# Two transformer blocks in float32: the second block's heads taken two by two, and the linear attention's pair mask stored for its diagonal blocks only

## The reference, cut to what matters

```python
# gated linear attention, per chunk of 64 tokens
diff = bcum[:, :, :, None, :] - bcum[:, :, None, :, :]
decay = jnp.exp(jnp.where(mask[:, :, None], diff, -jnp.inf))
att = jnp.einsum('bhtd,bhsd,bhtsd->bhts', qc, kc, decay)
o_intra = jnp.einsum('bhts,bhse->bhte', att, vc)

# second block: A, 4 heads: the difference of two softmaxes with width 64
w = p[0] - lam * p[1];   oa = rms_norm(w @ v)
# B, 8 heads: a window of 128 tokens, with a sink
# C, 8 heads: three attentions (selected, window, compressed blocks), each with its own gate
out = g[..., 0:1] * o_cmp + g[..., 1:2] * o_sel + g[..., 2:3] * o_win
gate = jax.nn.sigmoid(mg)          # 3 x 1024 gates for each token
x = x + jnp.sum(gate * y, axis=2) @ w_out
```

## Time and profile before

| | us |
|---|---|
| median of 3 runs | 4096.61 |
| lowest and highest | 4095.42, 4098.13 |
| the profiled execution's own time | 4089.71 |
| its span, first to last instruction | 4087.9 |

### The profile page before, as it was taken

One profiled execution on the slowest core, in us unless ns is written; L12 is line 12 of the kernel. 1 busy time (PEld: TensorE's weight loads), 2 busy tenths in 40 slices (PEclk: granted clock), 3 DMA queues, 4 the chain that ended last, 5 costly groups with the idle time before them and its releaser, 6 DMA issues. The chain is left out here.

```text
span 4087.9 us, 51442 instructions
## 1 busy us (share of the span) xinstructions
PE 3835.9 (94%) x19551; PEld 3010.5 (74%) x19551; DVE 1891.2 (46%) x2849; ACT 1006.2 (25%) x1824; POOL 1965.8 (48%) x834
## 2 busy tenths in 40 slices
PE   7999999999988998899999999899899999999999
PEld 4777778888877887676678778677585555567877
DVE  3344336556547884244426556456214444463200
ACT  3333112222210001243312222101214444412200
POOL 3333342332335564344454443689443333287886
PEclk9999999999999998999999999999889999999999
DMA  6211221121125553222232222335422222253333
GB/s 207 50 44 48 75 50 42 44 50 42 45 75 118 115 106 108 72 55 56 55 85 55 63 61 51 89 91 140 123 57 69 64 55 68 62 159 78 93 92 92
DMA packets 485314, 317.41 MB, mean 78 GB/s; under 512 B 38185, under 2 KB 456370, under 8 KB 483210
## 3 DMA queue, kind: packets, MB, share of 16 engines
q1 hardware_dynamic: 466080, 288.14, 28.6%
q10 hardware_dynamic: 19050, 26.75, 1.9%
HBM read 282.25 MB, written 32.56 MB: 77 GB/s over the span
## 5 line engine op out<-in xcount | busy, mean ns | idle before, releaser
L945 POOL TENSOR_TENSOR whi<-ring,con 128x1024 fp32r<-128x1024 f32 (+1 forms) x415 | 980.1, 2362 | 2067.1 <-DMA ring<-in_w_in 1596.5
L622 PE MATMUL ps<-xT_parts,whi 128*128 128x512 f32 (+2 forms) x2632 | 1017.2, 386 | 71.7 <-DVE zz L2235 21.1
L622 PE MATMUL ps<-hT_parts,whi 128*128 128x512 f32 (+1 forms) x2864 | 1049.9, 367 | 0.0
L947 POOL TENSOR_TENSOR ring_parts<-ring,whi 128x1024 fp32r<-128x1024 f32 (+1 forms) x415 | 988.9, 2383 | 32.5
L622 PE MATMUL ps<-xT_parts,ring_parts 128*128 128x512 f32 (+2 forms) x2600 | 946.2, 364 | 0.0
L622 PE MATMUL ps<-arena_parts,whi 128*128 128x512 f32 (+1 forms) x2344 | 723.0, 376 | 50.5 <-DVE arena_parts L2267 37.0
L1659 ACT ACTIVATE arena<-ps 128x768 f32<-128x768 f32 (+9 forms) x561 | 298.7, 542 | 1625.9 <-PE ps L622 786.0
L622 PE MATMUL ps<-arena 128*128 128x128 f32 (+9 forms) x3292 | 644.6, 340 | 13.0 <-DVE arena L2235 9.5
L622 PEld LDWEIGHTS ps<-xT_parts,whi 128*128 128x128 f32 (+1 forms) x2632 | 501.2, 190 | 179.0 <-issue 87.9
L622 PEld LDWEIGHTS ps<-hT_parts,whi 128*128 128x128 f32 x2864 | 544.3, 190 | 89.6 <-issue 7.2
L622 PEld LDWEIGHTS ps<-arena 128*128 128x128 f32 (+3 forms) x3292 | 440.4, 194 | 168.3 <-issue 131.4
(11 more groups left out here) (173 smaller groups left out, 3617.7 us busy)
## 6 DMA issues: line engine op xcount, KB each, us to landing
ring<-in_w_in SPq DMA_DIRECT2D x504, 256.0 KB, 4.1
arena<-in_w_ada SPq DMA_DIRECT2D x64, 256.0 KB, 5.8
ring<-in_w_up SPq DMA_DIRECT2D x64, 256.0 KB, 4.0
ring<-in_w_down SPq DMA_DIRECT2D x64, 256.0 KB, 3.9
ring<-in_w_out SPq DMA_DIRECT2D x48, 256.0 KB, 3.9
gates_kept<-stage ACTq DMA_DIRECT2D x24, 384.0 KB, 3.9
arena<-gates_kept SPq DMA_DIRECT2D x24, 384.0 KB, 3.6
arena<-in_w_ada SPq DMA_DIRECT2D x8, 1024.0 KB, 20.0
```

The lines of the kernel that those rows point to most:

```text
L622: return nc.tensor.matmul(o, l, r, start=first, stop=last)
L945: v.tensor_tensor(hi, raw, ones[:, 0:m].unsqueeze(1).to_broadcast([P, kt, m]), ALU.mult).then_inc(w_rounded, 1)
L947: v.tensor_tensor(ringR[:, s, 0:kt, 0:m], raw, hi.bitcast(F32), ALU.subtract).then_inc(w_split, 1)
```

## The change

It does two things.

**1. Linear attention.** `pairs` is stored without its zero blocks (448 columns for each direction instead of 1024). `levels` makes one 64x64 matmul for the first halving, into bank 6, and then for the six others and the diagonal two matmuls each of 64 weight columns and 64 moving columns, one for each half, into 448 columns of bank 5. It waits for `att_ready` besides `masked`. `mask` multiplies 448 columns, sums over seven, spreads the 64 columns to the two blocks by a product with `blk`, and copies the corner.

**2. Heads.** Group 0 and group 1 of the same query tile now stand next to each other in `heads2`, and all engines go through it two scores at a time. `scores` issues two matmuls in a row, then come fill steps, the two turns, the values, and fill steps again. `values` takes both groups in turn, matmul by matmul, and sel and win apart. `pT2` has another layout with room for four uses. The planner works by pairs. Gate 0's tile is made before the first score, and its weights are loaded before SyncE waits for the phase "cmp" and issues the bias tables. The gates are kept as sigmoids, made with Exp, Ln and Exp instead of Tanh, so that one table serves the stage and it is loaded once before the heads; the branch stage then multiplies by the gate alone.

```diff
-        pairs.append(k.transpose(1, 0, 2).reshape(P, -1))
+        own_pairs = np.concatenate([k[1:8, :64, :64], k[1:8, 64:, 64:]], axis=1)
+        pairs.append(own_pairs.transpose(1, 0, 2).reshape(P, -1))
...
-            for kind, g, subs in (("A", 0, ("c",)), ("B", 0, ("b",)), ("B", 1, ("b",)),
-                                  ("C", 0, ("sel", "win", "cmp")), ("C", 1, ("sel", "win", "cmp"))):
...
+            for kind, sub, groups in (("A", "c", (0,)), ("B", "b", (0, 1)), ("C", "sel", (0, 1)), ("C", "win", (0, 1)),
+                                      ("C", "cmp", (0,)), ("C", "cmp", (1,))):
+                for qt in range(LT):
...
+                    for g in groups:
...
-        VALUES_AT = [("A", 0, 8, 2), ("B", 0, 17, 2), ("B", 1, 19, 2), ("C", 0, 28, 3), ("C", 1, 40, 3)]
+        VALUES_AT = [("A", 8, 2), ("B", 16, 2), ("sel", 24, 2), ("win", 32, 2), ("cmp0", 36, 1), ("cmp1", 40, 1)]
...
-        FILL_TILES, gates_planned = [], 0
+        FILL_TILES, gates_planned = [], 1
...
+            for p in range(pairs_):
+                spent += sum(pair_us(2 * p))
+                room = int((share * (p + 1) - spent) / step_us)
+                for slot in range(2):
+                    for _ in range(room - room // 2 if slot == 0 else room):
+                        if at == steps or 2 * p + slot < free:
+                            break
...
+                            ends[tile] = p
+                            free = 2 * p + (4 if FILL_TILES[tile][0] == "query" else 2)
...
                     for c in range(4):
                         load_query(0, c)
+                    load_gate(0)
...
                             pe.wait_ge(masked, f0 + f)
+                            pe.wait_ge(att_ready, f0 + f)
+                            halves = [slice(0, 64), slice(64, P)]
+                            keys_of = [gkE[:, j % 2, lv * P:(lv + 1) * P] for lv in range(LEVELS)]
+                            queries_of = [gqE[:, j % 3, lv * P:(lv + 1) * P] for lv in range(LEVELS)]
+                            mm(bank(6, 64)[halves[d]], keys_of[0][:, halves[d]], queries_of[0][:, halves[1 - d]], True, True)
+                            keys_of.append(gk[:, t * P:(t + 1) * P])
+                            queries_of.append(gq[:, t * P:(t + 1) * P])
                             for lv in range(LEVELS):
-                                mm(bank(5, 1024)[:, lv * P:(lv + 1) * P], gkE[:, j % 2, lv * P:(lv + 1) * P],
-                                   gqE[:, j % 3, lv * P:(lv + 1) * P], True, True)
-                            mm(bank(5, 1024)[:, 7 * P:8 * P], gk[:, t * P:(t + 1) * P], gq[:, t * P:(t + 1) * P],
-                               True, True).then_inc(att_done, 1)
+                                for half in halves:
+                                    last = mm(bank(5, LEVEL_COLS)[half, lv * 64:(lv + 1) * 64], keys_of[lv + 1][:, half],
+                                              queries_of[lv + 1][:, half], True, True)
+                            last.then_inc(att_done, 1)
...
-                mm(b, q, k, True, True).then_inc(scores2, 1)
+                return score_bank(n, u["w"]), q, k
+
+            def scores(n):
+
+                for b, q, k in [operands(n + c) for c in range(2)]:
+                    mm(b, q, k, True, True).then_inc(scores2, 1)
...
+                elif kind in ("sel", "win"):
+                    for s in range(LT):
+                        for g in range(2):
+                            todo.append((bank(1)[rows[g], s * P:], (vS if kind == "sel" else vW)[:, s, rows[g]],
+                                         pT_keys(use[g], s, s * P, LAT - s * P), kind == "sel" and s == 0, False))
...
-                        pe.wait_ge(gate2_tanh, before.count("gate"))
+                        pe.wait_ge(gate2_read, 1 + before.count("gate"))
...
+            pe.wait_ge(w_split, splits.number() + 1)
+            for k in range(KT):
+                fill_step(k)
             pe.wait_ge(n2_ready, NORM0 + 4)
...
+            scores(0)
+            for n in range(0, 4 * NS2 + 2, 2):
+                if n + 2 < 4 * NS2:
+                    scores(n + 2)
                 fill(n)
-                for q in ended(n - 1, "query"):
+                for m in (n, n + 1):
+                    if m < 4 * NS2:
+                        turn(m)
+                for m in (n, n + 1):
+                    for kind, first, steps in VALUES_AT:
+                        j, o = divmod(m - first, NS2)
+                        if 0 <= j < 4 and o < steps:
+                            values(j, kind, o, steps)
+                fill(n + 1)
+                for q in ended(n // 2 - 1, "query"):
                     pe.wait_ge(fill_kept, q + 1)
                     pe.wait_ge(sq2_ready, NORM0 + 4 + q + 1)
                     mm(bank(2), blk, n2sq, True, True).then_inc(ms2_done, 1)
...
+            log_and_exp_table()
             for c in range(4):
                 normed2(NORM0 + c)
...
+            def gate_value(g):
+
+                product()
+                if g >= 2:
+                    act.wait_ge(gate2_kept[g % 2], 16 * (g // 2))
+                value = gate_out2[g % 2]
+                do(value, bank(2).rearrange("p (a n) -> p a n", a=2), ACT.Exp, scale=-1.0).then_inc(gate2_read, 1)
+                act.wait_ge(gate2_read, g + 1)
+                do(value, value, ACT.Ln, bias=one).then_inc(gate2_ln, 1)
+                act.wait_ge(gate2_ln, g + 1)
+                do(value, value, ACT.Exp, scale=-1.0).then_inc(gate2_ready, 1)
+                tiles.next()
...
+            gate_value(0)
             exp(0)
             exp(1)
+            keep_gate2(0)
+            for n in range(0, 4 * NS2, 2):
...
-                    log_and_exp_table()
...
+                for g in ended(n // 2 - 1, "gate"):
+                    gate_value(g)
+                if n + 2 < 4 * NS2:
+                    exp(n + 2)
+                    exp(n + 3)
                 copy(n)
...
+                copy(n + 1)
...
-                        v.tensor_tensor(gam, bank(5, 1024).rearrange("p (l t) -> p l t", l=8), pairs[:, d],
-                                        ALU.mult).then_inc(masked, 1)
+                        v.tensor_tensor(gam, bank(5, LEVEL_COLS), pairs[:, d], ALU.mult).then_inc(masked, 1)
                         dve.wait_ge(masked, f0 + f + 1)
+                        own(v.tensor_reduce(gdiag, gam.rearrange("p (l t) -> p t l", l=LEVELS), AX.X, ALU.add))
+                        own.settle()
 
                         dve.wait_ge(o_done, f0 + max(f - 1, 0))
-                        v.tensor_reduce(gatt[:, f % 2], gam.rearrange("p l t -> p t l"), AX.X, ALU.add).then_inc(att_ready, 1)
+                        own(v.tensor_tensor(gatt[:, f % 2].rearrange("p (c t) -> p c t", c=2),
+                                            gdiag.unsqueeze(1).to_broadcast([P, 2, 64]),
+                                            blk.rearrange("p (c t) -> p c t", c=2), ALU.mult))
+                        own.settle()
+                        rows, cols = slice(64 * d, 64 * d + 64), slice(64 * (1 - d), 64 * (1 - d) + 64)
+                        v.tensor_copy(gatt[rows, f % 2, cols], bank(6, 64)[rows]).then_inc(att_ready, 1)
...
+            for n in range(0, 4 * NS2, 2):
                 i, m = divmod(n, NS2)
+                normalise(n)
+                normalise(n + 1)
                 if n + 2 < 4 * NS2:
                     maximum(n + 2)
-                normalise(n)
+                    maximum(n + 3)
...
-                release(stt(pieces[0], gate_in2[g % 4], 1.0, pieces[1], ALU.add, ALU.mult))
+                release(v.tensor_tensor(pieces[0], gate_in2[g % 4], pieces[1], ALU.mult))
```

More of the change, by code:

```diff
@@ L38 @@
 SUM_COLS = LEVEL_COLS + 2 * 128
-CON_ROOM = 2 * (9 * 128 - SUM_COLS)
+CON_ROOM = 2 * (9 * 128 - SUM_COLS) + 2 * (8 * 128 - LEVEL_COLS)
 NEG = -1e30
@@ L136 @@
 for _n, _w in (("ident", P), ("ones", P), ("blk", P), ("anti", P), ("rot", P), ("cos", LAT), ("sin", LAT),
-               ("sums", 2 * SUM_COLS), ("pairs", 2 * 8 * P), ("room", CON_ROOM)):
+               ("sums", 2 * SUM_COLS), ("pairs", 2 * LEVEL_COLS), ("room", CON_ROOM)):
     C_AT[_n] = (_at, _w)
@@ L566, in two_blocks, with pair_us @@
                     gates_planned += 1
[L568 to L579, removed]
+        def pair_us(n):
+            scores = 2 * (heads2[n + 2]["w"] / 1200 + 0.1) if n + 2 < 4 * NS2 else 0.0
+            others = 0.0
+            for m in (n, n + 1):
+                if m < 4 * NS2 and heads2[m]["sub"] != "c0":
+                    others += 0.1 + 0.11 * -(-heads2[m]["w"] // P)
+                for kind, first, steps in VALUES_AT:
+                    j, o = divmod(m - first, NS2)
+                    if 0 <= j < 4 and o < steps:
+                        others += {"A": 1.1, "B": 0.6, "sel": 0.7, "win": 0.7}.get(kind, 0.9)
+            return scores, others
@@ L581, in planned_fill @@
         def planned_fill():
-            step_us, units = 0.7, 4 * NS2 - 4
```

(26 more changed lines are left out.)

152 lines of the change are left out of this document (71 added, 81 removed).

## The result

The changed kernel takes 3971.4 us (median of 4 runs, 3961.6 to 3975.7) beside 4096.0 for the kernel before on the same chip: a ratio of 0.9692, 95% interval 0.9673 to 0.9711. I had forecast 3949; 148 us were to go and 125 went. The profiled execution has a span of 3970.8 us (before 4087.9, so 117.1 in the two traces).

A forecast was written before the change was run, and what follows sets the result against it. TensorE, busy for 94% of the span, was taken to bound the kernel. Gains of 86 + 3 + 45 + 14 = 148 us were to bring the median from 4096.6 to 3949 us, range 3915 to 4020.

The forecast's parts named there:

- the overlap of halves: Heads, TensorE: matmuls on the array's two halves run side by side; 33 us for scores, 24 us for values.
- the visits saved: Heads: leaving full-size matmuls and coming back costs 0.33 us; 80 fewer for scores, 26 us, and 3 us for values.
- scores 59 forecast: Heads, scores: 33 us for columns behind their twins plus 26 us for 80 returns to full-size matmuls saved.
- values 24 forecast: Heads, values of B, sel and win: 3456 columns for each i vanish behind their twins, 24 us.
- 89: Heads of block 2, whole stage: 86 us of TensorE's work plus 3 us from moving gate 0's tile.
- a term of 86: Heads: TensorE's gain from scores and values together, 86 us.
- the gates' tile: Heads, gates: the 6.5 us that TensorE waited for the tanh were to stay.
- rival 2: Heads: a pair's softmax chain takes over; pairs 0.6 us longer give back 48 us, 3997; chance 0.13.
- my sign: Trace after: heads from first score to last copy in about 390 us, TensorE still over 93% busy.
- Rival 1: Linear attention: small pairs of levels run in series, losing 18 us instead of gaining 45; 4012 us; chance 0.16.
- a term of 45: Linear attention, TensorE: levels takes 1.23 us instead of 1.79 in each of 80 units, 45 us gained.
- 14 us on VectorE's side: Linear attention: shorter mask and sum gain 8 us at zz waits and some 6 us after last full units.

The follow-up runs named there:

- the second execution: The changed kernel, unchanged, run once more against the kernel before: 3960.6 us beside 4085.7, ratio 0.9700.
- The sum in PSUM: The changed kernel with the sum of the levels written to PSUM, so the spread reads one SBUF operand: 3955.9 us, ratio 0.9662 of the kernel before.
- the kernel with both cures: The changed kernel with the corner copied first, two short reductions replacing the spread, and levels waiting only for the mask's product: 3957.8 us, ratio 0.9676.

## Why the prediction was right, and where it was wrong

**Right.** TensorE bounds the heads, and the overlap of halves and the visits saved there were worth what the terms say: scores 59 forecast, 56 measured in the stage; values 24 forecast, 25 measured by blocks. The surplus of 8 us over 89 lies in TensorE's busy time (490.3 to 395.3 us for a term of 86), not in its idle time (23.3 and 21.6). Of it 3 to 5 us are that one trace of before, and the granted clock rose from 0.96 to 0.99, which the sum had at nothing. In the idle time two steps were wrong and cancelled. TensorE's wait for the gates' tile, which was to stay, fell from 6.5 us to 1.6. And a wait that the sum did not have grew from 0.9 us to 9.5, a wait that the profile puts down to nobody and calls "issue", after:

```profile
PE ps L638 <- issue: 9.5, 10, 1.4
```

All ten, and the two of before, end 0.09 us after ScalarE has read a query tile's mean square out of bank 2 (`ms2_read` in the trace). The work that the plan puts there does not cover it. That much of rival 2 was there; the rest stayed away, since TensorE's waits for normalisations came to 4.3 us (4.7 before). From the first score to the end of the stage 376 us passed, where my sign said about 390. The stretch ahead of it grew from 34.3 us to 40.7 (36.4 in the second execution) for gate 0's tile. Rival 1 fell with `levels` at 1.15 us. A unit of the linear attention shortened from 8.47 to 7.97 us in the first layer and from 7.05 to 6.53 in the second (medians from one transposed key to the next): 80 x 0.51 = 41 us for a term of 45.

**Wrong** is the last step of the linear attention: "The new wait of `levels` for `att_ready` of the unit before holds nothing: VectorE ends that a whole unit earlier, 7 to 8 us". It counted from the end of `levels`, and the mask is not next on VectorE's queue then. The scaled keys and queries of the next unit stand ahead of it, and these wait for ScalarE's exponentials of sums that TensorE makes just ahead of `levels`. By the rows above ScalarE takes 1.34 us from its start to VectorE's (2266.83 to 2268.17), and VectorE then needs 2.46 us for the scaling, 1.87 for the mask without its spread and 2.24 for the held spread, up to 2274.74. That is 7.91 us from one `levels` to the end of the mask that the next `levels` waits for, and a unit of the second layer takes 6.53: late, as the wait of 1.56 us shows. With a spread of 0.29 it would be 6.0, and in time. In the first layer, with units of 7.97, even a held spread ends in time, and the waits for the corner copy are 1.2 us in all, with the hold and without. I should have laid ScalarE's and VectorE's work along one unit of the shorter layer, which the wait added to the kernel before shows to be tight already.

**Mis-sized** was the spread, bounded by a product of one PSUM and one SBUF operand (0.28): the row has the right width and the wrong operands. With it the term "14 us on VectorE's side" came out at 4 us in the first layer (the `zz` waits fell from 21.1 to 17.2, mean 2.15 and not 1.6) and negative in the second.

Together: 23 us short of 148 by the medians. By stages of the two traces (31 us short), 28 are in the second linear attention and 4 in the first, 7 were lost in stages that the change does not touch, and the heads gave 8 more than forecast. The 28 are 12 of busy time and 16 of idle time: TensorE was to be busy 18 us less and was 5.8 (443.1 to 437.3; 16.8 in the second execution, at the clock of before), and it was to idle 5 us less and idled 10.8 more. Of the 16 the hold has 8 (31.0 without it in place of 38.9), 5 are waits for the corner copy that stay without the hold, and 3 were not parted. What stays open is the 7: the longest of these stages alone (421.1 us before, 425.5 after) lies between 417 and 432 us in kernels with the same instructions there, with the clock at 0.95 to 0.92, and no run tells what sets it.

The sum in PSUM is the fastest version measured: 0.9662 of before. Its interval overlaps that of the changed kernel's first measurement (from 0.9673) and just misses that of the second (from 0.9681); what stands behind it is the idle time of the second linear attention, 31.0 us against 38.7 to 40.9.

## What to carry to other kernels

Before costing a small VectorE instruction by its columns, look where its operands live: with both in SBUF it lasted up to 2.3 us beside a GpSimd pass instead of 0.29, and with one of them in PSUM 0.29 each time. A new wait is judged on the queue of the engine that ends it, over one period of the shortest stage, not by when its input is ready. A neighbour in the other half of TensorE's array was nearly free here, even for matmuls of 64 columns (30 passes in 1.15 us, 1.78 with the halves parted). And where one execution of a stage differs from the next by its clock, compare TensorE's idle time too.

## What the runs showed of the hardware

- The hold reaches the smallest instructions. In the heads, after, a product of single columns took 1.23 us beside a GpSimd pass from 3201.77 to 3204.16; of the 32 instances of this line 16 start while such a pass runs and take 0.51 to 1.99, and the 16 others take 0.15 or 0.16:

```profile
3200.34 0.15 DVE L2885 TENSOR_TENSOR small<-small 128x1 f32<-128x1 f32 x1
...
3201.77 2.39 POOL L962 TENSOR_TENSOR whi<-ring,con 128x1024 fp32r<-128x1024 f32 x1 [6.46 <-DMA ring<-in_w_in]
...
3202.95 1.23 DVE L2885 TENSOR_TENSOR small<-small 128x1 f32<-128x1 f32 x1 [0.41 <-ACT ps L1699]
```

- A plain copy from SBUF to SBUF is held too (5 of 80 corner copies in the kernel that copies it first, all beside a pass); the reductions from SBUF to SBUF and the memset in the kernel with both cures never were (80 of each, 21 to 26 beside a pass).
- Column halves of TensorE take work out of order with respect to each other: four passes of one half ahead in the program did not delay the other half's; with eight ahead it started beside the fifth; a full-width matmul parts them.
- The same instructions of one stage took 466 to 476 us, with granted clocks of 0.99 to 0.97, and TensorE idled 38.7 to 40.9 us in each.
